# Two blocks of a projection before the norm instead of one: weights times x that is not yet normed, at five norms of a two-block network

## The chip, the cores and the metric

The kernel runs on one core of one Trainium2 chip. What counts is the time of one execution on the device in microseconds. Of three runs of the kernel before the median is 1563.91 us (1560.41 to 1564.23). Engines are named as in the profile: TensorE is PE, its weight loads PEld, VectorE is DVE, ScalarE is ACT, GpSimd is POOL, SyncE (SP) issues the weight transfers.

## The reference

One sequence of 256 tokens with 1024 features goes through two blocks. All of it is float32. The first has a convolution branch and a state-space branch, then a gated feed-forward part. The second has a gated-delta mixer (gdn) and a gated-linear mixer (gla), each followed by a squared-relu MLP. Cut to the places that the change touches:

```python
# first block
x = x + gate * (merged @ w_out)                      # w_out
h = rmsnorm(x) * (1 + scale) + shift                 # norm "ffn"
u = h @ w_ffn_in;  x = x + gate * ((silu(u1) * u2) @ w_ffn_down)
x = rmsnorm(x) * final_norm_w                        # norm "final"
# second block, i = 0 (gdn) and 1 (gla)
m = mixer_i(x)                                       # first projection: a_qkv, b_qk
x = layernorm(ALPHA * x + m)                         # norms "ln1_0", "ln1_1"
a = relu(x @ mlp_w1)                                 # mlp1_0, mlp1_1
x = layernorm(ALPHA * x + (a * a) @ mlp_w2)          # norms "ln2_0", "ln2_1"
```

## The kernel before, in words

The 256 tokens lie along the free axis, features on the partitions: x is the tile X of eight 128x256 pieces. A projection is a **section** (the list SECS): a series of 256-column blocks of weights. SP loads a block of 1 MB (8 k-tiles of 128 rows) into one of four slots of `raw`, in one order for the whole kernel (`order`), as soon as the block four places earlier has been used. Float32 precision comes from splitting weights and data in two: ScalarE makes the high part `whi` (split_hi, L463), VectorE or, in the sections with lo="gpsimd" (a_qkv is one), POOL makes the low part `wlo` (split_lo, L473), which also frees the raw slot. A block has two tiles of 128 columns (h = 0, 1); `whi` and `wlo` have four places, so two blocks. TensorE multiplies each k-tile three times (L596 hi x hi, L597 hi x lo of the data, L598 lo x hi): 48 matmuls a block, summed in one of four PSUM slots `acc` (out_slot). Some engine then evacuates the tile (acc_free).

In ffn_in some raw slots hold parts of w_ada_ffn instead (ADA_PLAN): after blocks 1, 3, 5 and 7 VectorE folds them into ADAG (L1678, L1680), which is what frees those slots.

**Norms.** Before a norm x is summed from the residual evacuations (L1971, L1975) of the section before: w_out, ffn_down, a_out, mlp2_0, b_out (BEFORE). Sections with several k-chunks per output (ffn_down, mlp2_0: four) are "long": only every fourth block ends in an evacuation. For five norms (EARLY) the first block of the next section (ffn_in, a_qkv, mlp1_0, b_qk, mlp1_1) does not wait: while the section before ends, ScalarE squares x (SQX) and writes its high part times the gain (GHI, act_first, L760, L761), VectorE the low part (GLO, low_halves, L794); TensorE (pe_early, L692, L714, L718) multiplies with these, with the sums over features for mean and variance between them (L697, L700, L703, L707), and two extra columns carry the gain and the shift through the weights. When the norm's factors NR are there, VectorE's scale_first (L857 to L864) corrects the two tiles of block 0 in PSUM.

The norm itself is norm_dve and norm_act: VectorE makes the low split of block 1 (L473), mean and variance (L928 to L931), centres x (L934, not for ffn and final), scales it (L940, SQX), runs scale_first and writes the low part HL (L954, L956); ScalarE loads a table (L880), makes the high split of block 1, the inverse root (L913, L916) and the high part HH (L907, L909). Block 1 is the first on HH: pe_first (L530, L531) does its hi matmuls as each HH piece comes, then those on HL (L537). After that split_section runs each engine through the blocks: split of block b + 1, then the evacuation of block b, then `extra`.

**What lies behind.** In a_qkv each tile is evacuated by ScalarE (L1422) and by four VectorE operations (conv, L1828); `gates` on VectorE (L2016 to L2021, with softplus, L1744 to L1756) stands after block 2's conv, and decay_sides(0) to (7) after those of blocks 3 to 10 (L2030 to L2034). L2505 on TensorE waits for the last of them. PE computes small_tok and the shift sums (pe_shift, L726, L727) after block 1. In mlp1_0 the shift sums stand after block 1, and POOL then adds the shift to X (L740). In b_qk the shift sums and the gate logits (L2684) stand after block 1, L2691 after block 2. b_v (L588) follows.

Of the kernel before, what the change touches and what calls it, by code (L numbers as in the profile page):

```python
# [20 lines left out]
P = 128  # L21
# [65 lines left out]
def program(nc, a, out):  # L87
# [46 lines left out]
    for k in ("conv_b", "conv_a", "xbc", "z", "g", "conv_out", "ssm_out", "w_out", "ffn_in", "a_qkv", "mlp1_0", "mlp1_1"):  # L134
        SEC[k].flat = True
# [70 lines left out]
    with ExitStack() as ctx:  # L206
# [77 lines left out]
        WB = at("WB", 101.75, [P, 4])  # L284
# [191 lines left out]
        def split_section(eng, split, s, evac, chain=None, per=0, extra=None):  # L476
# [29 lines left out]
        def out_slot(s, u, h):  # L506
# [6 lines left out]
            return (s.o0 + h) % 4  # L513

        def pe_first(pe, s, rhs, ready, b, u, j):

            hi_part, lo_part = ready
            for h in range(2):
                pe.wait_ge(hi_ready, 2 * b + s.t0 + h + 1)
                pe.wait_ge(raw_used, 2 * (b + s.w0) + h + 1)  # L520
                if s.name == "ffn_in":
                    pe.wait_ge(acc_free, s.o0 + 2 * h + 2)
# [28 lines left out]
        def pe_block(pe, s, rhs, tok_major=False, free=None, ready=None):  # L551

            def body(b, u, last, j, only=(0, 1)):
                k = kt_of(s, u)
                if s.name in NORM_OF and b == 0:
                    pe_early(pe, NORM_OF[s.name])
                    return
                if ready and b == (1 if s.name in NORM_OF else 0):
# [4 lines left out]
                for h in only:  # L563
                    tt = 2 * b + s.t0 + h
                    pe.wait_ge(hi_ready, tt + 1)
                    pe.wait_ge(raw_used, 2 * (b + s.w0) + h + 1)
                    if first:
# [8 lines left out]
                        else:  # L576
                            pe.wait_ge(acc_free, 2 * j + s.o0 + h + 3)
                    slot, q = (s.t0 + 2 * u + h) % 4, out_slot(s, u, h)
# [46 lines left out]
        for n, (name, mean, src) in enumerate(norm_list):  # L625
# [8 lines left out]
        PARTS = {"ffn": 0, "final": 1, "ln1_0": 2, "ln2_0": 4, "ln1_1": 6}  # L634
        RANK = {name: i for i, name in enumerate(EARLY)}
        BEFORE = {"ffn": "w_out", "final": "ffn_down", "ln1_0": "a_out", "ln2_0": "mlp2_0", "ln1_1": "b_out",
                  "ln2_1": "mlp2_1"}

# [30 lines left out]
        def parts(name):  # L669

            if SEC[BEFORE[name]].chunks > 1:
                return [NR[:, 0]], [SQX[:, 0]]
            return [XP[:, i] for i in range(3)], [SQX[:, i] for i in range(3)]

        def width(name):
            return T if name == "final" else WIDE

        def pe_early(pe, name):
# [3 lines left out]
            place_ = [(h, (s.t0 + h) % 4, out_slot(s, 0, h)) for h in range(2)]  # L682
            for h in range(2):
                pe.wait_ge(hi_ready, s.t0 + h + 1)
                pe.wait_ge(raw_used, 2 * s.w0 + h + 1)
            late = 2 if SEC[BEFORE[name]].chunks > 1 else 0
# [2107 lines left out]
```

## Time and profile before

| | before |
|---|---|
| median of 3 runs | 1563.91 us |
| profiled execution | 1569.33 us, span 1567.6 us |
| PE busy | 1430.1 us (91%) |
| DVE busy | 1011.0 us (64%) |
| ACT busy | 773.8 us (49%) |
| POOL busy | 404.8 us (26%) |
| granted TensorE clock, mean | 0.959 |
| DMA | 223.74 MB, 143 GB/s |

Shares are means over stages with different limits. The chain that ended last runs through PE for 72% of the span, through DVE for 13%, ACT for 6%. The five places lie at 453 to 475 us (ffn), 650 to 712 (final), 963 to 988 (ln1_0), 1161 to 1209 (ln2_0) and 1348 to 1373 (ln1_1) of the span. All times below count from the span's start.

### The profile page before, as it was taken

The page shows a single profiled execution, that of the slowest core. Times are in us where ns is not written, and L with a number is a line of the kernel's source. Part 1 is how long each engine was busy: PE and PEld are TensorE (multiplying, and loading weights), DVE is VectorE, ACT ScalarE, POOL GpSimd, SP SyncE. Part 2 cuts the span into 40 slices and gives each one's busy share as a digit, 9 for nine tenths or more (in the row PEclk, how much of TensorE's full clock was granted, in tenths as well). Part 3 has the DMA queues.
Part 4 walks back from the last instruction along what each step waited for, and adds up shares of the span by engine and source line. Part 5 has one row for each costly group of instructions (what it writes and reads, how often), then busy time and mean ns, then how long its engine had stood idle before and what let it go on. Part 6 is the DMA issues. An engine that isn't in the chain of part 4 may idle for free.

```text
span 1567.6 us, 27516 instructions
## 1 busy us (share of the span) xinstructions
PE 1430.1 (91%) x10981; PEld 1376.4 (88%) x10981; DVE 1011.0 (64%) x1726; ACT 773.8 (49%) x1211; POOL 404.8 (26%) x362
## 2 busy tenths in 40 slices
PE   4979999989898999898988889999999987999998
PEld 4979999988898999898878879999997976899997
DVE  6687868657676655579655557865464565876442
ACT  3424465574363433464573545664354643666333
POOL 1566774304300000156372401730005000200000
PEclk9889999999899999989999999999999998999999
DMA  9944553233746745635310005555552510365540
GB/s 354 363 135 148 175 162 108 82 107 120 240 153 221 227 158 161 202 85 159 108 54 1 1 1 161 158 183 171 187 161 83 179 38 14 122 188 189 176 146 28
DMA packets 202480, 223.74 MB, mean 143 GB/s; under 512 B 7608, under 2 KB 197723, under 8 KB 200317
## 3 DMA queue, kind: packets, MB, share of 16 engines
q1 hardware_dynamic: 201072, 220.67, 43.8%
q8 instruction: 80, 1.31, 0.4%
q10 hardware_dynamic: 1293, 1.47, 0.3%
q14 instruction: 35, 0.29, 0.1%
HBM read 221.07 MB, written 1.05 MB: 142 GB/s over the span
## 4 chain that ended last, share of the span: by engine, by line
PE 72%; DVE 13%; ACT 6%; POOL 3%; issue 3%; DMA 2%; SPq 0%; DVEq 0%; ACTq 0%; POOLq 0%
PE acc L596 18%; PE acc L598 17%; PE acc L597 17%; DVE GB L1828 2%; DVE wlo L473 1%; ACT whi L463 1%; POOL H L967 1%; PE acc L537 1%; PE acc L530 1%; DMA raw<-in_w_ffn_in 1%; DVE SQX L940 1%; DMA XIN<-in_x 1%; PE acc L531 1%; POOL AM L1194 1%; PE pm L2359 1%
## 5 line engine op out<-in xcount | busy, mean ns | idle before, releaser
L596 PE MATMUL acc<-HH,whi 128*128 128x256 f32 x1744 | 501.2, 287 | 29.1 <-issue 9.1
L463 ACT ACTIVATE whi<-raw 128x1024 fp32r<-128x1024 f32 (+2 forms) x380 | 378.7, 1029 | 242.1 <-PE acc L598 194.1
L597 PE MATMUL acc<-HL,whi 128*128 128x256 f32 x1744 | 496.0, 284 | 0.0
L598 PE MATMUL acc<-HH,wlo 128*128 128x256 f32 x1744 | 495.9, 284 | 0.0
L473 DVE TENSOR_TENSOR wlo<-raw,whi 128x1024 fp32r<-128x1024 f32 (+2 forms) x292 | 340.0, 1196 | 208.5 <-ACT whi L463 205.8
L596 PEld LDWEIGHTS acc<-HH,whi 128*128 128x128 f32 x1744 | 334.4, 192 | 36.6 <-issue 28.6
L597 PEld LDWEIGHTS acc<-HL,whi 128*128 128x128 f32 x1744 | 334.0, 192 | 0.3 <-issue 0.2
L598 PEld LDWEIGHTS acc<-HH,wlo 128*128 128x128 f32 x1744 | 333.6, 191 | 0.0
L473 POOL TENSOR_TENSOR wlo<-raw,whi 128x1024 fp32r<-128x1024 f32 x88 | 213.6, 2446 | 397.9 <-DVE wlo L473 246.6
L596 PE MATMUL acc<-HIDH,whi 128*128 128x256 f32 x688 | 195.7, 284 | 6.4 <-ACT whi L463 4.5
L597 PE MATMUL acc<-HIDL,whi 128*128 128x256 f32 x688 | 195.4, 284 | 0.0
L598 PE MATMUL acc<-HIDH,wlo 128*128 128x256 f32 x688 | 195.3, 284 | 0.0
L596 PEld LDWEIGHTS acc<-HIDH,whi 128*128 128x128 f32 x688 | 132.7, 193 | 7.0 <-issue 7.0
L597 PEld LDWEIGHTS acc<-HIDL,whi 128*128 128x128 f32 x688 | 132.9, 193 | 0.0
L598 PEld LDWEIGHTS acc<-HIDH,wlo 128*128 128x128 f32 x688 | 132.8, 193 | 0.0
L1814 DVE SCALAR_TENSOR_TENSOR pm<-UP,par,pm 128x256 f32<-128x256 f32 x158 | 66.9, 481 | 0.0
L530 PE MATMUL acc<-HH,whi 128*128 128x256 f32 x128 | 40.9, 342 | 15.7 <-ACT HH L909 6.7
L1561 ACT ACTIVATE TMP<-acc 128x256 f32<-128x256 f32 x60 | 23.0, 384 | 63.8 <-PE acc L598 58.9
L1194 POOL TENSOR_TENSOR AM<-ATT,gm 128x512 f32<-128x512 f32 x28 | 38.4, 1394 | 59.3 <-DVE ATT L2114 42.0
L2195 DVE TENSOR_TENSOR TMQ<-TMP 128x256 f32<-128x256 f32 x64 | 28.9, 452 | 37.4 <-ACT HIDH L1564 37.4
L1828 DVE SCALAR_TENSOR_TENSOR GB<-acc,par,GB 128x254 f32<-128x254 f32 (+1 forms) x96 | 45.1, 480 | 9.2 <-ACT GB L1422 6.4
L967 POOL TENSOR_SCALAR X<-SQX,par 128x256 f32<-128x256 f32 x8 | 8.2, 1035 | 161.0 <-DVE SQX L940 161.0
(554 smaller groups left out, 2541.7 us busy)
## 6 DMA issues: line engine op xcount, KB each, us to landing
raw<-in_mlp_w SPq DMA_DIRECT2D x64, 1024.0 KB, 5.3
raw<-in_w_in SPq DMA_DIRECT2D x36, 1024.0 KB, 5.3
raw<-in_w_ffn_in SPq DMA_DIRECT2D x22, 1024.0 KB, 5.3
raw<-in_a_w_in SPq DMA_DIRECT2D x16, 1024.0 KB, 5.7
raw<-in_b_w_in SPq DMA_DIRECT2D x12, 1024.0 KB, 5.3
raw<-in_w_ada_mix SPq DMA_DIRECT2D x8, 1024.0 KB, 7.1
ADR<-in_w_ada_ffn SPq DMA_DIRECT2D x8, 1024.0 KB, 11.5
raw<-in_w_ssm_out SPq DMA_DIRECT2D x8, 1024.0 KB, 5.2
```

The source lines that it names most:

```text
L463: act.activation(whi[:, (s.t0 + 2 * u + h) % 4, 0:k], raw[:, place(s, b, u) % 4, 0:k, h * P:h * P + P], ACT.Copy).then_inc(hi_ready, 1)
L473: v.tensor_tensor(wlo[:, slot, 0:k], raw[:, place(s, b, u) % 4, 0:k, h * P:h * P + P], whi[:, slot, 0:k].bitcast(F32), ALU.subtract).then_ ...
L530: pe.matmul(acc[:, q, 0:T], whi[:, slot, i], hh, start=i == 0, stop=False)
L596: pe.matmul(acc[:, q, 0:T], whi[:, slot, i], hh, start=first and i == 0, stop=False)
L597: pe.matmul(acc[:, q, 0:T], whi[:, slot, i], hl, start=False, stop=False)
L598: m = pe.matmul(acc[:, q, 0:T], wlo[:, slot, i], hh, start=False, stop=final and i == k - 1)
L967: pool.tensor_scalar(dst[:, k], SQ[name][:, k], shift(k) if shift else 0.0, None, ALU.add)\
L1194: pool.tensor_tensor(AM[u][:, lv % 2].rearrange("p (s c) -> p s c", s=4), ATT[u][:], mask, ALU.mult).then_inc(am_ok, 1)
L1561: act.activation(TMP[:, q], acc[:, out_slot(s, u, h), 0:T], ACT.Relu, bias=evac_bias(s, b, u, h))\
L1814: c.tick(v.scalar_tensor_tensor(ACC[:, i] if w_ == CW - 1 else sum_, src, wt, sums.get(i, sum_), ALU.mult, ALU.add))
L1828: ins = v.scalar_tensor_tensor(d_, x_, pc(w, i + 24 * tap), d_, ALU.mult, ALU.add)
L2195: c.link(v.tensor_tensor(TMQ[:, q], TMP[:, q], TMP[:, q], ALU.mult))
```

## The change

Blocks 0 and 1 of the five sections are now both multiplied with GHI and GLO in pe_early; the first block on HH is block 2. WB grows to eight columns, scale_first gets a block number and runs twice, for block 0 ahead of HL and for block 1 behind it. ScalarE's table load and the high splits of blocks 0 and 1 move ahead of the last evacuations; the high split of block 2 comes after HH. VectorE makes the low split of block 1 after the variance, of block 2 between scale_first(0) and HL, and of block 3 in block 1's turn of split_section. The order of pe_early changes: hi and lo weights on the first six k-tiles, and the last two last. Of the sums, the parts over the first k-tiles (pe_parts) are multiplied before the last tile of the section before, and short sections have one summed part each instead of three. `mid` runs between the two last residual evacuations, so that pieces 6 and 7 of x are handled one by one; the low halves of a long section are made in two groups of three. ffn_down and mlp2_0 become `flat` (written out, not looped) and rotate their output tiles over four slots. The first three low splits of a_qkv go from POOL to VectorE. gates, small_tok, the shift sums and the gate logits come one block later, and so do decay_sides; act_shift of mlp1_0 two.

```diff
-    for k in (..., "w_out", "ffn_in", "a_qkv", "mlp1_0", "mlp1_1"):
+    for k in (..., "w_out", "ffn_in", "ffn_down", "a_qkv", "mlp1_0",
+              "mlp2_0", "mlp1_1"):
...
                 for h in range(2):
-                    if s.name in NORM_OF and eng is not nc.gpsimd and b == 0:
+                    if s.name in NORM_OF and b in (0, 2):
                         continue
-                    if split and not last:
+                    if split and s.name in NORM_OF and b == 1:
+                        split(eng, s, 3, 3, h)
+                    elif split and not last:
                         split(eng, s, b + 1, u + 1, h)
...
                         evac(b, u, h, j)
+                        if mid and last and h == 0:
+                            mid()
...
-            return (s.o0 + h) % 4
+            return (s.o0 + h + (2 * j if s.flat else 0)) % 4
...
-                if s.name in NORM_OF and b == 0:
-                    pe_early(pe, NORM_OF[s.name])
+                if s.name in NORM_OF and b < 2:
+                    if b:
+                        pe_early(pe, NORM_OF[s.name])
                     return
-                if ready and b == (1 if s.name in NORM_OF else 0):
+                if ready and b == (2 if s.name in NORM_OF else 0):
                     pe_first(pe, s, rhs, ready, b, u, j)
...
+                    if s.name in NORM_BEFORE and last and h == 1:
+                        pe_parts(pe, NORM_BEFORE[s.name])
...
+            tiles = [(2 * b + h, (s.t0 + 2 * b + h) % 4, out_slot(s, b, h)) for b in range(2) for h in range(2)]
...
+            open_(first)
+            with_hi(first, whi, range(6))
             if mean:
...
+            with_hi(first, wlo, range(6))
...
             m.then_inc(n_sum, 1)
...
+            open_(second)
+            with_hi(second, whi, range(6))
+            pe.wait_ge(raw_used, 2 * s.w0 + 2)
+            with_hi(second, wlo, range(6))
+            for tile in (first, second):
+                with_lo(tile, range(6))
+            for tile in (first, second):
+                with_hi(tile, whi, (6, 7))
+                with_hi(tile, wlo, (6, 7))
+                with_lo(tile, (6, 7)).then_inc(w_used, 1)
+            for tile in tiles[2:]:
+                open_(tile)
+                with_hi(tile, whi, range(8))
+                with_lo(tile, range(7))
+                pe.wait_ge(raw_used, 2 * s.w0 + tile[0] + 1)
+                with_hi(tile, wlo, range(8))
+                with_lo(tile, (7,)).then_inc(w_used, 1)
...
+                if b == last - 1:
+                    act.preload_act_table_set("natural_log_exp_and_others")
+                    for h in range(2 if name == "ffn" else 0):
+                        split_hi(act, e, 0, 0, h)
+                elif b == last:
+                    split_hi(act, e, 1, 1, 0)
+                    act_first(act, name, (6, 7))
+                    split_hi(act, e, 1, 1, 1)
...
+                if b == last - 1 and name in ("ffn", "final"):
+                    v.wait_ge(raw_used, 2 * e.w0)
+                    for h in range(2):
+                        split_lo(v, e, 0, 0, h)
+
+            def mid():
+                if not is_long(name):
+                    v.wait_ge(n_sq, 8 * n + 6)
+                    v.tensor_tensor(SQX[:, 4], SQX[:, 4], SQX[:, 5], ALU.add).then_inc(part_ok, 1)
+                low_halves(v, c, name, (6,))
...
+            if name in EARLY:                      # norm_act, at its end
+                for h in range(2):
+                    split_hi(act, SEC[EARLY[name]], 2, 2, h)
...
+            if e:                                  # norm_dve, after the variance
+                for h in range(2):
+                    split_lo(v, e, 1, 1, h)
...
-            if name in EARLY:
-                scale_first(v, c, name)
+            if e:
+                scale_first(v, c, name, 0)
+                for h in range(2):
+                    split_lo(v, e, 2, 2, h)
             for k in range(DT):                    # HL
...
+            if e:
+                scale_first(v, c, name, 1)
...
-            lo_section(SEC["a_qkv"])
+            s = SEC["a_qkv"]
+            for b in range(3, s.nb):
+                if b == 3:
+                    pool.wait_ge(raw_used, 2 * (s.w0 + b))
+                for h in range(2):
+                    split_lo(pool, s, b, b % 4, h)
...
-                if b == 2:
+                if b == 3:
                     gates()
-                elif 3 <= b < 11:
-                    decay_sides(b - 3)
+                elif 4 <= b < 12:
+                    decay_sides(b - 4)
```

## Rows read from the trace of the kernel before

**Rows 1.** TensorE's waits over the span: waiter, releaser, us in total, times, longest.

```profile
PE acc L530 <- ACT HH L909: 6.7, 4, 2.8
...
PE acc L596 <- DVE GB L1828: 5.1, 1, 5.1
PE acc L692 <- DVE X L1975: 4.9, 1, 4.9
```

**Rows 2.** Windows of TensorE alone: us, busy (instructions), granted clock, DMA share, GB/s.

```profile
990.00:1060.00 70.00, 70.00 (x592) 1.00 0.62 194
1184.00:1187.00 3.00, 3.00 (x16) 0.50 0.14 19
```

**Rows 3.** Timeline of DVE at the norm ffn: start, us, what, [idle before <-releaser].

```profile
457.08 2.36 DVE L473 TENSOR_TENSOR wlo<-raw,whi 128x1024 fp32r<-128x1024 f32 x2 [1.77 <-ACT whi L463]
459.35 3.25 DVE L940 SCALAR_TENSOR_TENSOR SQX<-X,MOD,NR 128x256 f32<-128x256 f32 x8
...
463.58 3.25 DVE L956 SCALAR_TENSOR_TENSOR HL<-SQX,MOD,HH 128x256 fp32r<-128x256 f32 x8
466.74 2.35 DVE L473 TENSOR_TENSOR wlo<-raw,whi 128x1024 fp32r<-128x1024 f32 x2
...
472.35 1.28 DVE L1680 SCALAR_TENSOR_TENSOR ADAG<-raw,cs,ADAG 128x1024 f32<-128x1024 f32 x1
```

**Rows 4.** The chain that ended last, in ffn_in: start, us, what.

```profile
473.66 5.17 DMA raw<-in_w_ffn_in
...
487.49 5.25 DMA raw<-in_w_ffn_in
```

**Rows 5.** Timeline of TensorE where that chain lets go.

```profile
516.58 0.36 PE L596 MATMUL acc<-HH,whi 128*128 128x256 f32 x1 [1.41 <-ACT whi L463]
```

**Rows 6.** Timeline of DVE in a_qkv, around gates.

```profile
696.06 0.38 DVE L2016 TENSOR_TENSOR spt<-pm,gab 128x16 f32<-128x16 f32 x2
...
698.71 7.84 DVE L1753 SCALAR_TENSOR_TENSOR spt<-spt,spt 128x32 f32<-128x32 f32 x7
...
709.88 3.98 DVE L1828 SCALAR_TENSOR_TENSOR GB<-acc,par,GB 128x254 f32<-128x254 f32 x8 [0.16 <-DVE gd L2021]
```

**Rows 7.** Timeline of POOL in the same stretch.

```profile
698.52 4.74 POOL L473 TENSOR_TENSOR wlo<-raw,whi 128x1024 fp32r<-128x1024 f32 x2 [11.08 <-ACT whi L463]
```

**Rows 8.** Timeline of TensorE behind a_qkv.

```profile
756.22 0.49 PE L2505 MATMUL pm<-maskf,LF 128*128 128x128 f32 x2 [2.22 <-DVE LB L2031]
```

**Rows 9.** Groups by line, 964 to 988 us: xcount | busy us, mean ns | idle before.

```profile
L697 PE MATMUL pm<-SQX,maskf 128*128 128x256 f32 x6 | 1.5, 379 | 0.0
```

**Rows 10.** Timeline of DVE at the norm ln1_0.

```profile
972.03 2.73 DVE L934 SCALAR_TENSOR_TENSOR X<-pm,X 128x256 f32<-128x256 f32 x8
974.68 4.28 DVE L940 SCALAR_TENSOR_TENSOR SQX<-X,par,NR 128x256 f32<-128x256 f32 x8
...
980.98 3.25 DVE L956 SCALAR_TENSOR_TENSOR HL<-SQX,par,HH 128x256 fp32r<-128x256 f32 x8
...
985.73 2.35 DVE L473 TENSOR_TENSOR wlo<-raw,whi 128x1024 fp32r<-128x1024 f32 x2
```

**Rows 11.** Timeline of TensorE at ln1_0: the shift sums follow block 1.

```profile
985.46 0.28 PE L726 MATMUL pm<-HH,maskf 128*128 128x256 f32 x1
```

**Rows 12.** Timeline of TensorE at ln1_1: the first matmul of block 2.

```profile
1372.25 0.36 PE L596 MATMUL acc<-HH,whi 128*128 128x256 f32 x1 [1.44 <-issue]
```

**Rows 13.** Timeline of TensorE at ln2_0.

```profile
1169.75 2.08 PE L718 MATMUL acc<-GLO_ln,whi 128*128 128x258 f32 x16
1174.63 0.36 PE L530 MATMUL acc<-HH,whi 128*128 128x256 f32 x1 [2.81 <-ACT HH L909]
...
1180.46 4.67 PE L537 MATMUL acc<-HL,whi 128*128 128x256 f32 x16 [0.60 <-DVE HL L956]
...
1187.94 3.64 PE L2684 MATMUL pm<-X,ws 128*32 128x256 f32 x16
```

**Rows 14.** Timeline of TensorE: the first matmul of b_v.

```profile
1209.02 0.39 PE L588 MATMUL acc<-whi,HH 128*128 128x256 f32 x1 [0.47 <-ACT QK L1580]
```

More of the change, by code:

```diff
@@ L133, in program @@
     SEC = {s.name: s for s in SECS}
-    for k in ("conv_b", "conv_a", "xbc", "z", "g", "conv_out", "ssm_out", "w_out", "ffn_in", "a_qkv", "mlp1_0", "mlp1_1"):
+    for k in ("conv_b", "conv_a", "xbc", "z", "g", "conv_out", "ssm_out", "w_out", "ffn_in", "ffn_down", "a_qkv", "mlp1_0",
+              "mlp2_0", "mlp1_1"):
         SEC[k].flat = True
@@ L633, in program @@
         XC0 = {"conv": 0, "ln1_0": 8, "ln2_0": 17, "ln1_1": 26, "ln2_1": 35}
-        PARTS = {"ffn": 0, "final": 1, "ln1_0": 2, "ln2_0": 4, "ln1_1": 6}
+        PARTS = {"ffn": 0, "final": 2, "ln1_0": 3, "ln2_0": 6, "ln1_1": 8}
         RANK = {name: i for i, name in enumerate(EARLY)}
@@ L667, in norm_pe, with is_long, pe_parts @@
                 keep_busy(pe, 4)
[L669 to L673, printed above, removed]
+        def is_long(name):
+            return SEC[BEFORE[name]].chunks > 1
         def width(name):
             return T if name == "final" else WIDE
+        def pe_parts(pe, name):
+            mean = NORM[name][1]
+            pe.wait_ge(part_ok, PARTS[name] + (2 if mean else 1))
+            if mean:
+                pe.matmul(pm[:, 0, 0:T], ones, NR[:, 0] if is_long(name) else XP[:, 0], start=True, stop=False)
+            pe.matmul(pm[:, 1, 0:T], ones, SQX[:, 0], start=True, stop=False)
         def pe_early(pe, name):
@@ L681, in pe_early, with with_hi, with_lo, open_ @@
             o0 = SEC[BEFORE[name]].o0 + 4
[L682 to L686, printed above, removed]
[L687 to L689 removed]
+            tiles = [(2 * b + h, (s.t0 + 2 * b + h) % 4, out_slot(s, b, h)) for b in range(2) for h in range(2)]
+            def with_hi(tile, weights, ks):
+                i, slot, q = tile
                 for k in ks:
                     pe.wait_ge(g_hi, g + k + 1)
[L692 to L697 removed]
+                    pe.matmul(acc[:, q, 0:w], weights[:, slot, k], hi[:, k, 0:w],
+                              start=k == 0 and weights is whi, stop=False)
+            def with_lo(tile, ks):
+                i, slot, q = tile
+                for k in ks:
+                    pe.wait_ge(g_lo, g + k + 1)
+                    m = pe.matmul(acc[:, q, 0:w], whi[:, slot, k], lo[:, k, 0:w], start=False, stop=k == 7)
+                return m
+            def open_(tile):
+                i = tile[0]
+                pe.wait_ge(hi_ready, s.t0 + i + 1)
+                pe.wait_ge(acc_free, s.o0 + i + 1)
+            first, second = tiles[0], tiles[1]
+            open_(first)
+            with_hi(first, whi, range(6))
             if mean:
[L699 to L700 removed]
                 for k in (6, 7):
@@ L704, in pe_early @@
                 m.then_inc(n_mean, 1)
+            pe.wait_ge(raw_used, 2 * s.w0 + 1)
+            with_hi(first, wlo, range(6))
+            if not is_long(name):
+                pe.wait_ge(part_ok, PARTS[name] + (3 if mean else 2))
+                pe.matmul(pm[:, 1, 0:T], ones, SQX[:, 4], start=False, stop=False)
             for k in (6, 7):
```

208 lines of the change are left out of this document (100 added, 108 removed).

## The prediction

> **What bounds the kernel now.** I read four views, in this order. First the waits of TensorE over the whole span: who ends its idle times. TensorE is the engine that is nearly always busy, so only its idle times, its slow stretches and work taken off it can move the end. Of the joints that the diff touches, the first block on the normed x waited for ScalarE's HH four times (6.7 us in all), GHI_final's first matmul waited 4.9 us for the last residual, and a_qkv waited 5.1 us once for VectorE [rows 1]. Second, windows: undisturbed, 592 matmuls take 70 us, 0.118 us each, so a block of 48 takes 5.7 us; in a disturbed stretch 16 fall in 3 us at a granted clock of 0.50, 0.19 to 0.21 us each [rows 2]. Third, VectorE's order of work around each norm, since it makes everything TensorE waits for there. Fourth, in ffn_in, the chain of waits, which does not run through TensorE at all: an ADAG step on VectorE frees a raw slot, a 5.2 us transfer fills it, ScalarE and VectorE split it, VectorE evacuates, and does the next ADAG steps [rows 4].
>
> **The plan of the change.** In each of five places TensorE gets 48 more matmuls (5.7 us) that need no norm and are moved ahead of the first block that does. Their total number stays. That covers the wait for HH. But VectorE is the engine that follows the norm, and it gets more to do before it is through: scale_first for a second block, and the low split of block 2 ahead of HL. So for each place I lay VectorE's row durations end to end in the new order and see what TensorE meets. Starts that no row gives are sums of such durations, good to about 1 us.
>
> **ffn.** Before: low split of block 1 (2.36), eight scalings (3.25), scale_first (1.0, from 462.60 to 463.58), eight HL (3.25), low split of block 2 (2.35, to 469.09), two evacuations and a first ADAG step (3.3), the second (1.3), which ends at 473.63 [rows 3]. In the new order a second scale_first (1.1) and the low split of block 3 (2.36) stand before that ADAG; the wait for the high split of block 2, which ScalarE now does after HH, adds 0.6; the table load, moved ahead of the first high split, and two small additions make the scalings start 0.3 late; block 1's split no longer waits. Sum 1.1 + 2.4 + 0.6 + 0.3 = 4.4, with link overheads 4.7: the ADAG ends near 478.3. TensorE itself would be 2 us early at the end of block 2. That is worth nothing: its next weights need the slot that this ADAG frees. The loop has a period of 13.8 us (473.66 to 487.49) for two blocks that cost TensorE 11.4, with no matmul in it [rows 4], and it only lets go at 516.58, where TensorE still idles 1.41 us before it [rows 5]. So the shift is carried through whole: **+4.7 us** (bounds 2.4, the moved split alone, and 6).
>
> **final.** The 4.9 us wait goes: VectorE no longer does six low halves and three sums in one piece ahead of the last residuals, and TensorE, with four rotating output slots, may start before them. POOL's low splits of blocks 0 and 1 go to VectorE, which is not blocked then. TensorE's sums end near 661.3, 132 matmuls follow (15.7 us), and block 2 is done near 677. But a_qkv is then VectorE's. gates() with its small operations took from 696.06 to 709.72, because each of the two-input ones met a POOL split: seven L1753 take 7.84 us, while the first two operations of gates, ahead of the split, take 0.38 together [rows 6, 7]. It is now done after conv of block 3 instead of block 2 (3.98 each, [rows 6]). VectorE's queue is: convs of blocks 0 to 3 from 677 on, 16 us, gates at 693.1, 13.7 us as before, end 706.9 against 709.7: 2.8 us won. From there to the last decay side, which releases L2505 at 756.22 [rows 8], the same eight convs and eight decay sides follow in either kernel, 46.5 us of VectorE, so L2505 comes 2.8 us earlier. No conv is behind it any more (it had been 3.97 us ahead of ScalarE's last silu and its exponentials), I take 1.2 us for that; TensorE idles longer before it, and I give back 0.7 for clock. **-3.3 us** (bounds 0 and -8, the latter if gates meets no POOL work).
> The Trainium skill ("SBUF — State Buffer", section "Who interferes with whom") says that VectorE and GpSimd take their common port as a lock for a whole instruction, and the later one is blocked: the rows of L1753 agree. By that rule what counts is which instruction POOL has running when gates comes.
>
> **ln1_0.** Three fewer sum matmuls (six instructions take 1.5 us, [rows 9]: 1.3 us off), and two of the rest moved before the last tile. The sums end near 969.0. TensorE then has 84 matmuls, 10.0 us: free at 979.0. VectorE: the low split of block 1 stays ahead of the centring (2.36, 2.73), scalings 4.28, scale_first 2.1, so until 981.0, as before; then the low split of block 2, its first half ready at 982.2 [rows 10]. **So TensorE's new wait is for a low split, 3.2 us.** Block 2 lasts until 988.0 (before, block 1 ended at 985.46 [rows 11]), and with the shift sums (1.9) block 2 is done at 989.9, against 985.46 + 1.9 + 5.7 = 993.1. Behind block 2's split VectorE has HL 3.25, scale_first 2.1, two evacuations 1.6 (984.2 to 985.73), then the split of block 3, first half at 991.7. Block 3 so starts 1.4 us early. The 3.2 us of idling will probably bring half clock for a while, which the wait at block 3 hides for the most part; POOL's X additions now meet a VectorE that is behind. I take **-0.7 us** (bounds -3 and +2).
>
> **ln1_1.** The same without shift sums: waits of 2.6 us before block 2 and 3.6 before block 3, which starts at 1376.4 where before it would have started at 1378.0 (block 2 at 1372.25 [rows 12] plus 5.7): -1.6, and 0.6 for clock. **-1.0 us** (-2 to +2).
>
> **ln2_0.** Before, TensorE idled 2.81 and 0.60 us, and its 16 lo matmuls took 4.67 instead of 2.08 [rows 13]; two slow stretches follow. Block 3 ended at 1208.5, the next block began at 1209.02 [rows 14]. After: sums at 1167.5, 84 matmuls until 1177.5, low split of block 2 at 1180.7 (scale_first 3.0 here), block 2 until 1186.5, shift sums 1.9, gate logits 3.6 [rows 13], block 3 (its split is ready at 1189.4, so no second wait) until 1197.8, L2691 3.8: 1201.6. That is 6.9 us early; half clock after the 3.2 us of idling costs 1.5 to 3. **-4.9 us** (-7 to -2).
>
> **At no cost.** ffn_down and mlp2_0 written out instead of looped: TensorE has no idle time in their loops, so there is nothing to win; if fetching code stalled once, it would cost 1 to 2 us. WB and the output slots take no time.
>
> **Sum.** +4.7 - 3.3 - 0.7 - 4.9 - 1.0 = -5.2 us. The profiled execution took 1569.33 us (span 1567.6), 5.4 above the median of the runs; so 1564.1 by its own count, and 1563.91 - 5.2 = 1558.7 for the median.
>
> **Rivals.**
> *VectorE eats the cover.* Slower. The place is the wait for the low split before blocks 2 and 3. If VectorE's queue (scale_first, split, HL, scale_first, evacuation) is longer by 2 us than I have it, in all five places, then ln1_0 and ln1_1 each cost 1, final gives 0, ln2_0 gives 2.5, and ffn costs 6: +5.5, 1569. It decides from where block 3 starts later than before, 1.4 us beyond my schedule of ln1_0. For it: the longest wait of the sort before was already VectorE's, 5.1 us in a_qkv [rows 1]. Against: the durations are plain rows of the same operations.
> *The slot chain gives way.* If ADAG's delay is caught up in ffn_in, that place gives -2 and not +4.7: 1552. For it: VectorE idles over 4 us per turn for the transfer. Against: the idling is inside the loop, and nothing else of the loop gets shorter [rows 4].
> *POOL is idle while gates runs.* Final gives -8: 1554. For it: TensorE runs two blocks ahead of VectorE, so POOL may be done. Against: ScalarE's exponential waits for gates, and its next high split stands behind it, so POOL starts within gates.
> *Clock.* [rows 2, 13] show half clock after idling of 3.4 us. My schedule has five waits of 2.6 to 3.6 us; at 1.5 us each, three not hidden beyond those that I counted: +4.5, 1563. The Trainium skill ("TensorE: Matmul & The Clock Gate", "HAM oscillation — how this bites in real kernels") speaks against waits of this sort between bursts; the rows agree.
>
> **Chances.** My forecast 0.45 (own range 1555 to 1563), VectorE 0.15, slot chain 0.10, POOL idle 0.15, clock 0.15. The range, 1551 to 1567, leaves out half of the slower case. About 0.3%, 4.7 us, is what a measurement of this kernel can tell from no change. Below 1559.2: 0.28 of my own case and the slot and POOL cases, 0.53. Above 1568.6 or near it: 0.12. The rest 0.35.
>
> **What would show it.** ADAG L1680 of block 1 ends near 478.3, and TensorE's wait at 516.58 comes 4 to 5 us late. No wait of L692 for X. TensorE's first matmuls on HH wait for wlo (VectorE), not for HH. gates ends near 707, L2505 starts near 753 plus the shift of ffn. b_v's first matmul comes some 5 us sooner after the end of mlp2_0. Wrong would be: an ffn_in that is not later, a ln2_0 without gain, or half clock throughout the third blocks.

## The result, and the profile after

The changed kernel is slower: 1581.05 us, median of four runs (1578.04 to 1586.44), against 1564.02 us for the kernel before; the ratio is 1.0109, 95% interval 1.0087 to 1.0131. My forecast was 1558.7, with a range of 1551 to 1567. The profiled execution took 1580.77 us, with a span of 1579.0. All medians here are of the fast runs; one slow run in ten of adag1 is left out.

From the page of the changed kernel: busy time (share of the span) and instructions by engine, then the granted clock in 40 slices.

```profile
PE 1419.7 (90%) x10967; PEld 1372.9 (87%) x10967; DVE 1021.2 (65%) x1770; ACT 772.6 (49%) x1211; POOL 392.1 (25%) x356
...
PEclk9889999999899999989899999999999998999999
```

TensorE is busy for 10 us less than before and the span is 11.4 us longer, so TensorE idles more. The waits of TensorE over the whole span say where (waiter, releaser, us in total, times, longest); of the first view of before, this is what answers to [rows 1]:

```profile
PE acc L604 <- ACT whi L464: 10.9, 4, 5.7
...
PE acc L535 <- DVE GB L1899: 9.4, 1, 9.4
PE acc L535 <- ACT TMP L1632: 9.1, 1, 9.1
...
PE pm L2581 <- DVE LB L2107: 7.3, 1, 7.3
```

The first matmuls on the normed x (now L535, block 2) hardly wait for this norm's HH any more (1.7 us once, L963, where the list of before has 6.7 for its L909). But two of them wait 9.4 and 9.1 us for the *evacuation of an output tile*, a releaser that is in none of my cases. L2581 (the L2505 of before) waits 7.3 us where it waited 2.2 [rows 8].

The two traces differ by 11.45 us. By the starts of the same instructions, one trace of each kernel, it falls to the stages so (us; the difference is that of the stage alone). The first mark is a residual evacuation of w_out, ahead of the norm ffn; L2505 and L2581 are the decay products, which wait for the last decay side.

| stage, up to | before | after | difference | forecast |
|---|---|---|---|---|
| ahead of the norm ffn | 446.41 | 448.42 | +2.0 | 0 |
| ffn, to ffn_down's first matmul | 594.57 | 600.14 | +3.6 | +4.7 |
| final, to L2505 / L2581 | 756.22 | 768.50 | +6.7 | -3.3 |
| ln1_0, to mlp2_0's first matmul | 1069.59 | 1087.04 | +5.2 | -0.7 |
| ln2_0, to b_out's first matmul | 1325.86 | 1335.67 | -7.6 | -4.9 |
| ln1_1, to mlp2_1's first matmul | 1454.46 | 1465.79 | +1.5 | -1.0 |
| mlp2_1 and the end | 1567.60 | 1579.05 | +0.1 | 0 |

The medians are 17 us apart, 5.5 more than the traces: the profiled execution of before happened to lie 5.3 us above its median, that of after at its median.

**final.** Timeline of VectorE (start, us, what, [idle before <-releaser]), of POOL and of TensorE in the changed kernel; it answers to [rows 6 to 8].

```profile
676.27 7.06 DVE L1016 TENSOR_TENSOR HL<-SQX,HH 128x256 fp32r<-128x256 f32 x8
683.26 0.75 DVE L920 TENSOR_TENSOR acc<-acc,NR 128x256 f32<-128x256 f32 x2
683.92 7.85 DVE L1899 SCALAR_TENSOR_TENSOR GB<-acc,par,GB 128x254 f32<-128x254 f32 x16
693.83 3.98 DVE L1899 SCALAR_TENSOR_TENSOR GB<-acc,par,GB 128x254 f32<-128x254 f32 x8 [2.05 <-ACT GB L1493]
704.61 2.04 DVE L1899 SCALAR_TENSOR_TENSOR GB<-acc,par,GB 128x254 f32<-128x254 f32 x4 [6.80 <-ACT GB L1493]
707.46 2.04 DVE L1899 SCALAR_TENSOR_TENSOR GB<-acc,par,GB 128x254 f32<-128x254 f32 x4 [0.81 <-ACT GB L1493]
709.41 0.46 DVE L2092 TENSOR_TENSOR spt<-pm,gab 128x16 f32<-128x16 f32 x2
...
676.65 5.07 POOL L474 TENSOR_TENSOR wlo<-raw,whi 128x1024 fp32r<-128x1024 f32 x2 [267.12 <-ACT whi L464]
...
686.20 0.55 PE L535 MATMUL acc<-HH,whi 128*128 128x256 f32 x1 [9.42 <-DVE GB L1899]
694.07 3.65 PE L2435 MATMUL pm<-ws,SQX 128*128 128x32 f32 x32
768.50 0.80 PE L2581 MATMUL pm<-maskf,LF 128*128 128x128 f32 x2 [7.27 <-DVE LB L2107]
```

Two early blocks fill all four output slots. Block 2 needs block 0's first slot, whose taps (the convolution's four VectorE operations per tile, L1899) stand on VectorE behind the low halves HL. So TensorE idles until 686.20. Its small products (L2435) and shift sums come after block 2 and ahead of block 3, and VectorE, which needs block 3's tiles before it may begin the gates, idles 2.05 + 6.80 + 0.81 us among the taps. The gates begin at 709.41, against 696.06. The low halves themselves are late too: two of the eight take 2.57 and 2.56 us beside POOL's split, the other six 0.42 each.

**ln1_0.** The same view of VectorE, ScalarE and TensorE there, answering to [rows 10, 11].

```profile
996.67 3.25 DVE L1018 SCALAR_TENSOR_TENSOR HL<-SQX,par,HH 128x256 fp32r<-128x256 f32 x8
...
1001.13 0.76 DVE L920 TENSOR_TENSOR acc<-acc,NR 128x256 f32<-128x256 f32 x2
...
1001.26 0.47 ACT L1632 ACTIVATE TMP<-acc,WB 128x256 f32<-128x256 f32 x1 [6.32 <-DVEq L2265]
...
1001.99 0.55 PE L535 MATMUL acc<-HH,whi 128*128 128x256 f32 x1 [9.06 <-ACT TMP L1632]
```

Here the slot is freed by ScalarE's relu of block 0, and that waits for DVEq L2265: an increment, `v.sem_inc(hid_lo, 4)`, that hands out four free places of TMP at the start of VectorE's mlp(0). It stands behind the whole norm, both scalings included. Block 0 had been scaled since 994.5. Before, block 1 found its slots free and nobody on the path waited for that increment.

**ffn.** The chain of waits there (start, us, what), which answers to [rows 4]:

```profile
477.70 0.77 DVE ADAG L1749
478.47 0.02 issue
478.49 1.30 DVE ADAG L1751
479.79 0.02 issue
479.80 5.07 DMA raw<-in_w_ffn_in
484.87 0.02 issue
484.90 1.06 ACT whi L464
```

**ln2_0 and ln1_1.** TensorE's waits ahead of block 2 are for low splits, as forecast; they answer to [rows 12, 13].

```profile
1196.52 0.56 PE L535 MATMUL acc<-HH,whi 128*128 128x256 f32 x1 [2.97 <-DVE wlo L474]
...
1377.36 0.36 PE L535 MATMUL acc<-HH,whi 128*128 128x256 f32 x1 [2.16 <-DVE wlo L474]
1386.94 0.36 PE L604 MATMUL acc<-HH,whi 128*128 128x256 f32 x1 [3.41 <-DVE wlo L474]
```

### The profile page after: what moved, and what is told of

The parts are those of the page before. It is cut to its first block, busy times and chain, and to the rows that moved or that the text cites. A ratio compares the mean times of both kernels' runs of the same rounds, so it can differ in the third digit from the quotient of the medians.

```text
span 1579.0 us, 27235 instructions
## 1 busy us (share of the span) xinstructions
PE 1419.7 (90%) x10967; PEld 1372.9 (87%) x10967; DVE 1021.2 (65%) x1770; ACT 772.6 (49%) x1211; POOL 392.1 (25%) x356
## 4 chain that ended last, share of the span: by engine, by line
PE 71%; DVE 15%; ACT 5%; POOL 3%; issue 3%; DMA 2%; SPq 0%; DVEq 0%; ACTq 0%; POOLq 0%
PE acc L604 17%; PE acc L605 16%; PE acc L606 16%; DVE wlo L474 2%; DVE GB L1899 2%; PE acc L535 1%; POOL H L1031 1%; PE acc L536 1%; PE acc L702 1%; DMA raw<-in_w_ffn_in 1%; ACT whi L464 1%; DMA XIN<-in_x 1%; PE acc L542 1%; DVE HL L1018 1%; DVE SQX L1000 1%
## 5 line engine op out<-in xcount | busy, mean ns | idle before, releaser
L604 PE MATMUL acc<-HH,whi 128*128 128x256 f32 x1664 | 480.1, 288 | 33.8 <-POOL wlo L474 8.1
L605 PE MATMUL acc<-HL,whi 128*128 128x256 f32 x1664 | 475.0, 285 | 0.0
L606 PE MATMUL acc<-HH,wlo 128*128 128x256 f32 x1664 | 473.9, 285 | 0.0
L474 DVE TENSOR_TENSOR wlo<-raw,whi 128x1024 fp32r<-128x1024 f32 (+2 forms) x298 | 347.8, 1199 | 190.8 <-ACT whi L464 187.4
L604 PEld LDWEIGHTS acc<-HH,whi 128*128 128x128 f32 x1664 | 319.9, 192 | 39.9 <-issue 29.2
L605 PEld LDWEIGHTS acc<-HL,whi 128*128 128x128 f32 x1664 | 319.9, 192 | 0.3 <-issue 0.2
L606 PEld LDWEIGHTS acc<-HH,wlo 128*128 128x128 f32 x1664 | 319.7, 192 | 0.0
L474 POOL TENSOR_TENSOR wlo<-raw,whi 128x1024 fp32r<-128x1024 f32 x82 | 198.0, 2433 | 424.0 <-ACT whi L464 420.6
L535 PE MATMUL acc<-HH,whi 128*128 128x256 f32 x128 | 41.3, 347 | 33.6 <-DVE GB L1899 9.4
L535 PEld LDWEIGHTS acc<-HH,whi 128*128 128x128 f32 x128 | 31.8, 248 | 35.5 <-issue 30.0
L1899 DVE SCALAR_TENSOR_TENSOR GB<-acc,par,GB 128x254 f32<-128x254 f32 (+1 forms) x96 | 45.1, 480 | 12.4 <-ACT GB L1493 9.7
L1265 POOL TENSOR_TENSOR AM<-ATT,gm 128x512 f32<-128x512 f32 x28 | 38.4, 1393 | 59.1 <-DVE ATT L2190 41.8
```

What stands on the lines that cost most here:

```text
L474: v.tensor_tensor(wlo[:, slot, 0:k], raw[:, place(s, b, u) % 4, 0:k, h * P:h * P + P], whi[:, slot, 0:k].bitcast(F32), ALU.subtract).then_ ...
L535: pe.matmul(acc[:, q, 0:T], whi[:, slot, i], hh, start=i == 0, stop=False)
L604: pe.matmul(acc[:, q, 0:T], whi[:, slot, i], hh, start=first and i == 0, stop=False)
L605: pe.matmul(acc[:, q, 0:T], whi[:, slot, i], hl, start=False, stop=False)
L606: m = pe.matmul(acc[:, q, 0:T], wlo[:, slot, i], hh, start=False, stop=final and i == k - 1)
L1265: pool.tensor_tensor(AM[u][:, lv % 2].rearrange("p (s c) -> p s c", s=4), ATT[u][:], mask, ALU.mult).then_inc(am_ok, 1)
```

## The experiments

Each kernel is an edit of the changed one. The table gives stages from one trace of each (us): ffn and final run from the first matmul on GHI to the marks of the table above, ln1_0 from the decay products to mlp2_0's first matmul. So final begins later here than in the table above, and what the change saves ahead of GHI_final (4.7 us; the wait of 4.9 us there is gone) lies outside it. The same code differs between traces by up to 0.6 us in ffn, 2.1 in final and 1.7 in ln1_0.

| kernel | ffn | final | ln1_0 | span |
|---|---|---|---|---|
| before | 141.5 | 93.1 | 313.4 | 1567.6 |
| after | 144.3 | 104.5 | 318.5 | 1579.0 |
| nop | 144.2 | 104.6 | 312.6 | 1572.6 |
| pms | 144.1 | 102.9 | 311.4 | 1569.1 |
| one | 140.1 | 91.8 | 314.6 | 1565.3 |
| ln2 | 140.2 | 91.9 | 314.6 | 1558.4 |
| gates1 | 144.6 | 93.2 | 318.3 | 1573.7 |
| adag1 | 139.3 | 102.4 | 318.8 | 1571.6 |
| pe1 | 144.4 | 97.1 | 319.0 | 1566.4 |
| dve1 | 144.1 | 100.4 | 317.8 | 1571.1 |
| fixed | 139.5 | 92.9 | 312.6 | 1553.0 |
| best | 139.9 | 91.1 | 311.3 | 1554.4 |
| fixed_pool | 139.9 | 87.5 | 310.9 | 1551.0 |

### nop: the increment goes ahead of the norm

```
+            v.sem_inc(hid_lo, 4)
             norm_dve(v, c, "ln1_0", par_col("ln1_g"), par_col("ln1_b"))
 ...
-                if k == 0:
-                    v.sem_inc(hid_lo, 4)
```

> The changed kernel with one edit: VectorE gives the first four counts of hid_lo before the normalisation of ln1_0 and not behind it. Theory A (the second early block has taken the last free output slots, so block 2 of mlp1_0 waits for block 0's relu, and that relu waits for these four counts, which stand behind VectorE's low halves and the scaling of block 1): TensorE's wait of 9.06 us ahead of line 535 in ln1_0 falls to about 3.8 us, that is to the low split of block 2 (its end was 996.75, TensorE was free at 992.93); the kernel gains 5 us, 1581 to about 1576. All other sections stay within 0.5 us. Rival B (VectorE's backlog as such): the wait stays above 8 us, no gain. Rival C (the half clock is the cost): as A, but the half-clock window at 998.1 goes with the wait and the gain is 7 to 8 us.

Measured: 1571.36 us, ratio to the kernel before 1.0056 (1.0025 to 1.0088). TensorE's wait in ln1_0, in the trace of this kernel:

```profile
995.61 0.36 PE L535 MATMUL acc<-HH,whi 128*128 128x256 f32 x1 [2.75 <-DVE wlo L474]
```

The wait is 2.75 us instead of 9.06, and its releaser is now the low split, the one that I had forecast for this place. The stage is 6.0 us shorter (318.5 to 312.6). Theory A holds here; rival B falls. That the matmul runs at 0.36 us and not 0.55 shows the half clock gone with the wait, so C's part is included in those 6 us, not beside them. The medians moved by 9.7 us, more than A's 5 and C's 8, while the two traces differ by 6.5; the changed kernel has only four runs (1578.04 to 1586.44). So the price of a cause is read from its stage here and below, and the medians only say that it is there.

### pms: block 0 in other banks

```
+        def out_tile(s, b, u, h):
+            return pm[:, 2 + h] if in_pm(s, b) else acc[:, out_slot(s, u, h)]
 ...
+                if in_pm(s, 0):
+                    pass
+                    pe.wait_ge(acc_free, SEC["a_qkv"].o0 + 4 + 2)
                     small_tok(ws2, SQX, ba_p)
```

> The changed kernel, but block 0 of a_qkv and of mlp1_0 lies in the two banks of the other PSUM tensor that are free there, so that block 2 finds its output slots free; everything else, the order on every engine too, is as changed (TensorE's small products into one of these banks wait for the evacuation of block 0 first). Theory A: the waits of 9.42 us (final) and 9.06 us (ln1_0) ahead of line 535 fall to about 0.5 and 3.8 us; in final block 2 then waits 2 to 3 us for the low halves of h, which end at 683.3, and VectorE begins the gates near 700 instead of 709.4. In all 9 plus 5 us less, 1581 to about 1567. Rival B (VectorE's backlog): the waits move one block on, block 3 waits for block 1's evacuation as long, and the total falls by less than 4 us.

Measured: 1573.13 us, ratio 1.0049 (1.0026 to 1.0071). In ln1_0 it does what nop does. In final the slot wait is gone, and the stage is only 1.6 us shorter, which is no more than the same code differs by. TensorE and VectorE there:

```profile
681.18 3.32 PE L551 MATMUL acc<-HL,whi 128*128 128x256 f32 x13 [1.20 <-DVE HL L1025]
687.16 1.03 PE L2444 MATMUL pm<-ws,SQX 128*128 128x32 f32 x4 [2.66 <-DVE GB L1908]
...
700.69 2.04 DVE L1908 SCALAR_TENSOR_TENSOR GB<-acc,par,GB 128x254 f32<-128x254 f32 x4 [5.91 <-ACT GB L1502]
703.54 2.04 DVE L1908 SCALAR_TENSOR_TENSOR GB<-acc,par,GB 128x254 f32<-128x254 f32 x4 [0.81 <-ACT GB L1502]
705.50 0.46 DVE L2101 TENSOR_TENSOR spt<-pm,gab 128x16 f32<-128x16 f32 x2
```

This was my theory's miss. The 9.4 us that the list of waits shows were not what held the stage: VectorE still idles 5.91 us for block 3's tiles, since on TensorE the small products and the shift sums still come before block 3: 6.9 us in the changed kernel, near 10 here, most of it at half clock (the 32 small products take 7.01 us instead of 3.65). (2.66 us of the delay is the wait that this edit itself adds.) Whoever wants to know what a stage costs has to ask what VectorE's gates wait for, not what TensorE waits for.

### one, ln2: how many early blocks, and where

Each use of "two blocks" takes its number from a table:

```
+    NB = {'ffn': 1, 'final': 1, 'ln1_0': 1, 'ln2_0': 1, 'ln1_1': 1}
 ...
-                if s.name in NORM_OF and b < 2:
+                if s.name in NORM_OF and b < NB[NORM_OF[s.name]]:
```

> The changed kernel with one early block per norm instead of two, in all five places; the other parts of the change stay (four rotating slots for the long sections, flat sections, residuals and sums tile by tile, the table load and the high split moved). Theory A (the second block is what costs, by 3.7 + 6.7 + 5.0 + 1.5 us, and brings 7.6 in ln2_0): the total is about 1564 to 1570, ffn, final and ln1_0 back at the spans of the kernel before within 2 us each, ln2_0 about 7 us longer than changed. Rival D (the other parts of the change cost too): above 1575.

> As the run with one early block everywhere, but two early blocks at ln2_0 alone. Theory A: 7 to 8 us less than that run, near 1558 to 1562, faster than both kernels. Rival: the gain in ln2_0 came from the longer lead that the slower sections before it had given the DMA; then this run is within 3 us of the one with one block everywhere.

Measured: one 1563.30 us, ratio 0.9987 (0.9970 to 1.0004); ln2 1556.89 us, ratio 0.9960 (0.9931 to 0.9990). The other parts of the change cost nothing and bring nothing, together, that can be told from no change; rival D falls. The second block costs 4.2 us in ffn, 12.7 in final and 3.9 in ln1_0, and brings its gain in ln2_0, 6.8 us in the traces and 6.4 in the medians. ln2 beats both kernels. Its ln2_0 stage is as long as the changed kernel's (249.0 and 248.6), so a longer lead of the DMA, that run's rival, is not what brings the gain.

### gates1, pe1, dve1: where the gates stand in a_qkv

pe1 has the first hunk (TensorE), dve1 the others (ScalarE and VectorE), gates1 all:

```
 def gates(b):                       # TensorE: small products, shift sums
-    if b == 2:
+    if b == 1:
 def qkv_more(b):                    # ScalarE
-    elif b == 3:
+    elif b == 2:
 def qkv_more(b):                    # VectorE
-    if b == 3:
+    if b == 2:
         gates()
-    elif 4 <= b < 12:
-        decay_sides(b - 4)
+    elif 3 <= b < 11:
+        decay_sides(b - 3)
```

> The changed kernel with one edit in a_qkv: the small products and shift sums of TensorE come after block 1, and ScalarE's and VectorE's gate work after block 2, the block numbers of the kernel before; two early blocks and the slots stay. The run with block 0 in other banks took the slot wait of final away and left the stage as long as it was (102.9 us from the first early matmul to the decay products, changed 104.5, one early block 91.8), so my theory of the slots has fallen for final. Theory E (the gates' place): VectorE bounds a_qkv from the gates to the last decay side, 59 to 60 us in every kernel, and the change made it begin the gates after block 3's taps, and block 3 itself comes behind 7.6 us of small products on TensorE. With the old place the gates begin near 696 instead of 709.4, the last decay side lies ahead of block 11's taps again, and the decay products start near 756 instead of 768.5: 11 to 13 us less in all. Rival B (VectorE's additional work, a scaling and two low splits, is what costs): less than 6 us.

> The changed kernel with half of the edit on the gates: TensorE's small products and shift sums come after block 1, the gate work of ScalarE and VectorE stays behind block 3. It parts the 11.3 us that the whole edit took from the stage final (104.5 to 93.2 us from the first early matmul to the decay products). Theory E says that both halves count: here the small products fill TensorE's wait for the output slots, block 3 follows block 2 at once, VectorE's taps of blocks 0 to 3 run almost without a gap, and the gates begin 4 us (one block's taps) later than with the whole edit: stage 95 to 97 us. Rival (only the engines' order behind the gates counts): 103 to 105 us.

> The other half: the gate work of ScalarE and VectorE behind block 2, TensorE's small products still behind block 2 as changed. TensorE still waits for block 0's taps, the small products end near 698 and the shift sums near 701 in the changed kernel's times, ScalarE's sigmoid follows, and the gates begin near 702 instead of 709.4: stage 98 to 99 us. Rival (TensorE's order is what counts): 103 to 105 us.

Measured: gates1 1566.41 us, ratio 1.0031 (0.9996 to 1.0065); stage 93.2 us. pe1 97.1 us and dve1 100.4 us, from one execution each; their bands were 95 to 97 and 98 to 99, so both halves count; dve1's 4.1 us are about twice the scatter of this stage, pe1's 7.4 more than three times. VectorE's taps and the start of the gates, first in pe1, then in dve1:

```profile
680.12 7.86 DVE L1899 SCALAR_TENSOR_TENSOR GB<-acc,par,GB 128x254 f32<-128x254 f32 x16
688.87 5.93 DVE L1899 SCALAR_TENSOR_TENSOR GB<-acc,par,GB 128x254 f32<-128x254 f32 x12 [0.89 <-ACT GB L1493]
695.59 2.04 DVE L1899 SCALAR_TENSOR_TENSOR GB<-acc,par,GB 128x254 f32<-128x254 f32 x4 [0.79 <-ACT GB L1493]
697.54 0.46 DVE L2092 TENSOR_TENSOR spt<-pm,gab 128x16 f32<-128x16 f32 x2
```

```profile
691.17 3.98 DVE L1899 SCALAR_TENSOR_TENSOR GB<-acc,par,GB 128x254 f32<-128x254 f32 x8 [2.18 <-ACT GB L1493]
700.42 0.38 DVE L2092 TENSOR_TENSOR spt<-pm,gab 128x16 f32<-128x16 f32 x2 [5.26 <-ACT bet L1507]
```

In pe1 TensorE does the small products while it would have idled for the slot, and the taps of blocks 0 to 3 run with 1.7 us of gaps: this is the packed queue on which my forecast for final rested. In dve1 the gates wait 5.26 us for ScalarE's sigmoid, which hangs on TensorE's late sums. With both, the slot wait is covered and the gates come a block earlier. The spans of gates1 and the changed kernel differ by only 5.3 us, since gates1's trace is 7.7 us longer in ln2_0, which this edit doesn't touch (see the last section).

### adag1: ffn's slot is freed first

```
+            def ffn_pre(b):
+                for n in SEC["ffn_in"].ada[b] if b == 1 else ():
+                    ada_rest(n - 8)
-            split_section(v, split_lo, SEC["ffn_in"], ffn_up, extra=ffn_more)
+            split_section(v, split_lo, SEC["ffn_in"], ffn_up, extra=ffn_more, pre=ffn_pre)
```

> The changed kernel with one edit in ffn_in: VectorE does the ADAG step of block 1 ahead of the low split of block 3 and of the two evacuations. Theory (the step frees the weight slot on which the next load waits): the step ends near 475 instead of 479.8, the wait of 5.75 us at 487.4 falls to about 1.5 us, although block 3 now waits 2 us for its low split, and ffn_down begins 3.5 to 4.5 us sooner than the 600.14 of the changed kernel. Rival (the load was late for another reason, its queue or the high split): less than 1 us.

Measured: 1571.96 us, ratio 1.0032 (1.0002 to 1.0063); the stage is 139.3 instead of 144.3 us. Two views of TensorE in this trace (timeline):

```profile
476.77 0.36 PE L606 MATMUL acc<-HH,whi 128*128 128x256 f32 x1 [2.54 <-DVE TMQ L2064]
489.04 0.36 PE L606 MATMUL acc<-HH,whi 128*128 128x256 f32 x1 [0.64 <-issue]
```

The wait of 5.75 us is gone. Block 3 waits 2.5 us, about as long as expected, but not for its low split: the releaser is TMQ L2064, the evacuation of block 1, so here too an early block's output slot holds TensorE. The stage gains more than that costs, 4.9 us for a forecast of 3.5 to 4.5, since the chain that sets it runs through the weight slot. The rival falls.

### fixed, best: what the causes add up to

fixed holds nop, gates1 and adag1; best holds nop and NB = 2 in ln1_0, ln2_0 and ln1_1, 1 in ffn and final.

> Three edits in one: the counts of hid_lo ahead of ln1_0's normalisation, the gates in their old place, and ADAG's step of block 1 first; two early blocks everywhere. If the three causes are separate their gains add, 6 + 12 + 4 us: 1581 to about 1559, as fast as or faster than the kernel before by 0.3%. If one lies behind another, above 1565.

> Two early blocks in ln1_0, ln2_0 and ln1_1 and one in ffn and final, with the counts of hid_lo first. From the runs so far, against the run with two blocks at ln2_0 alone (1556.9): ln1_0 2 us less, ln1_1 1 us less, about 1554, that is 0.7% faster than the kernel before. Rival (the second block in ln1_0 and ln1_1 is worth nothing): 1557.

Measured: fixed 1556.45 us, ratio 0.9944 (0.9924 to 0.9963); best 1555.23 us, ratio 0.9928 (0.9903 to 0.9953). The three causes are separate: each stage of fixed is as in the run with its own edit, and against the changed kernel the three stages give 4.8 + 11.6 + 5.9 = 22.3 us of the 26.0 between the spans, for a forecast of 22. Most of the rest is ln2_0, 2.8 us shorter in this trace. The change, with three statements in other places, is faster than the kernel before. The intervals of fixed and best overlap, so which is better is not settled; 1555.23 also lies between best's forecast of 1554 and its rival's 1557 and decides for neither.

### fixed_pool: POOL waits for VectorE's low halves

```
                 if b == 3:
                     pool.wait_ge(raw_used, 2 * (s.w0 + b))
+                    pool.wait_ge(n_hl, 8 * HN["final"] + 8)
```

> The kernel with the three edits, and POOL begins its low split of block 3 of a_qkv only when all low halves of h are there. If POOL's running split is what makes VectorE's eight low halves take 7.07 us instead of 3.25, they take 2.8 to 3.3 us now, TensorE's wait of 3.0 us for them goes, and the gates begin 3 us sooner: 1556.5 to about 1553.5. Rival: POOL's split only moves onto something else that VectorE does with two inputs from SBUF, and the total stays within 1 us.

Measured: 1551.64 us, ratio 0.9907 (0.9879 to 0.9935). That is the lowest median of all, from four runs; the interval still overlaps those of fixed and best, so what shows the gain is the stage. VectorE and POOL in its trace:

```profile
670.30 2.77 DVE L1018 TENSOR_TENSOR HL<-SQX,HH 128x256 fp32r<-128x256 f32 x8
673.64 11.95 DVE L1902 SCALAR_TENSOR_TENSOR GB<-acc,par,GB 128x254 f32<-128x254 f32 x24
685.50 0.38 DVE L2098 TENSOR_TENSOR spt<-pm,gab 128x16 f32<-128x16 f32 x2
...
673.20 4.76 POOL L474 TENSOR_TENSOR wlo<-raw,whi 128x1024 fp32r<-128x1024 f32 x2 [262.75 <-DVE HL L1018]
```

The eight low halves take 2.77 us where they took 7.07 beside POOL's split. The gain, 4.8 us in the medians and 5.4 in the stage, is more than the 3 that I expected: the gates begin 5.8 us sooner after the first early matmul than in fixed, 4.3 us from the low halves and the rest from a gap of 1.58 us among the taps, which now run all 24 on end. TensorE's wait of 3.03 us for the low halves is gone. POOL's split runs beside the taps (L1902) and does not slow them: those that lie beside it take 0.47 to 0.49 us each, and so do those behind it. The taps have one input in PSUM, the low halves both in SBUF. The Trainium skill ("SBUF — State Buffer", section "Who interferes with whom") says this: two SBUF inputs on VectorE contend with a GpSimd instruction that reads SBUF, one input doesn't. Both rows agree.

## Why the prediction was wrong

The two traces differ by +11.4 us where the sum gave -5.2. Of these 16.7 us, 10.0 are final's and 5.9 are ln1_0's; the other stages err by 2.0, -1.1, -2.7 and 2.5 and nearly cancel.

**final, the step that failed: "convs of blocks 0 to 3 from 677 on, 16 us, gates at 693.1".** I queued VectorE's taps end to end, as if TensorE were ahead of it. My 677 is about 682.5 on the time axis of the changed trace (the sums end 5.5 us later there), so the gates should have begun at 698.6; they began at 709.41, 10.8 us later. VectorE's gaps among the taps are 9.7 us, the taps' late start 1.4. The gaps come from two things that I didn't lay out. First, TensorE's block 2 needs block 0's output slot. My sum let its 48 matmuls follow the 84 early ones at once ("132 matmuls follow (15.7 us), and block 2 is done near 677"); it was done at 694.1, 11.6 us after that place of the changed axis. I wrote that the slots "take no time" because I had looked at the rotation in ffn_down and mlp2_0 alone; in the places with two early blocks it is the other way round, all four are full. Second, I never placed the small products (3.65 us) and the shift sums between block 2 and block 3 in a_qkv, although I did so for ln1_0 and ln2_0. The trace of before had the warning: its taps stand still behind the same small work, too (timeline of VectorE in the kernel before):

```profile
691.26 2.04 DVE L1828 SCALAR_TENSOR_TENSOR GB<-acc,par,GB 128x254 f32<-128x254 f32 x4 [5.63 <-ACT GB L1422]
```

pe1, in which both fall into the gap, starts the gates at 697.54, with the early matmuls 3.8 us sooner than in the changed kernel: 2.7 us off my schedule. What follows the start of the gates was right: gates took 13.7 us as before, and from their start to the decay products it took 59.1 us, where before it was 60.2 and the forecast 59.8.

A third thing is missing in the sum. I took POOL's splits of blocks 0 and 1 away as a relief for VectorE; before, one of them had stretched the eight scalings (5.97 us instead of 3.25). But its split of block 3 now meets the low halves, and fixed_pool shows what that costs: 5.4 us of the stage.

The share of each: TensorE's part put back brings 7.4 us of final (pe1), the other part 4.1 (dve1), both 11.3. Taking the slot wait alone away brought 1.6, within the scatter of 2.1, and at most 4.3 if the 2.66 us that this edit adds are counted back. So the order of the small work is shown as the cause of most of the 11.3; the slot wait counts because that work stands behind it.

**ln1_0, the step that failed: "So TensorE's new wait is for a low split, 3.2 us."** True once the slot is free: 2.75 us in nop, and the stage is then 0.8 us shorter than before, for a forecast of -0.7; with a scatter of 1.7 us that agrees but doesn't confirm it. What I missed is a wait that is nobody's data: relu's permission to use TMP, an increment that stands behind the norm in VectorE's order. The list of waits of before showed no such releaser on TensorE, because block 1 had free slots of its own.

**ffn: right.** ADAG's step of block 1 ended at 479.8, forecast 478.3 and 2.0 for what came late ahead of the norm; the stage +3.6, forecast +4.7; and adag1 shows that this step's place is the cause.

**ln2_0: right in kind, the size not settled.** The wait is 2.97 us (forecast 3.2) on the split that I named, and the gain 7.6 (forecast 4.9, bounds 2 and 7). What I took off for clock is what varies most. Windows of TensorE behind that wait, in the changed kernel and then in gates1, 233 matmuls each (us, busy, granted clock, DMA share, GB/s):

```profile
1196.00:1231.00 35.00, 33.97 (x233) 0.95 0.39 121
```

```profile
1184.00:1223.00 39.00, 38.41 (x233) 0.83 0.35 108
```

In one trace a mean of 0.95 and 35 us, in the other 0.83 and 39: after the same wait the chip ran longer at 1.2 GHz instead of 2.4. Over the whole stage it is more. It takes 256.3 us in before and 255.8 in one; in the eleven traces with two early blocks at ln2_0 it takes 245.8 (fixed) to 256.3 (gates1), with a median of 248.9. So the gain is 7 us as a rule, 10 at best, 4 in best and fixed_pool, and nothing in gates1, though all wait 2.8 to 3.0 us in that place. My bounds of 2 and 7 were too narrow on both sides, and the 7.6 of one trace is not the size of the gain.

**ln1_1: not settled.** Forecast -1.0, measured +1.5. The waits are as forecast (2.16 and 3.41 us for 2.6 and 3.6). From b_out's first matmul to mlp2_1's, before took 128.6 us; the changed kernel and its edits with two blocks there took 127.8 to 130.4, those with one block at ln1_1 129.5 and 129.6, in the middle of the rest.

**The rivals.** "VectorE eats the cover" came nearest in time (1569) and named "the wait for the low split before blocks 2 and 3". But it priced two more microseconds of work in each of five places; what the runs show is an order of work, in final and in ln1_0. Its test, block 3 later than before in ln1_0, was met for another reason. None of the rivals had the output slots in it, and so the chance of a slower kernel, 0.12, was too small: I had listed what fills VectorE and not what each engine *holds* while it waits.

## What to carry to other kernels

Work pulled ahead of a dependency keeps its output buffer until the dependency is met: count the slots that it holds, and follow the next user of each slot back to its evacuation, over every semaphore that the evacuating engine waits for, those that only hand out permission too. When a block is added ahead of a section, everything that hangs on a block number behind it (small products, gates, increments) moves by a block in the order of its engine; place each again rather than adding to the numbers. And a long wait in the list of waits is not yet the price of a stage: take it away without changing anything else, and see whether the end moves.

## What I had not expected of the hardware

A POOL split of 5.07 us (two instructions, 2.58 and 2.52) stretches VectorE's eight two-input low halves from 2.77 to 7.06 us, and not evenly: two of them take 2.57 and 2.56, about one POOL instruction each, six stay at 0.42. Taps with one PSUM input stay at 0.47 to 0.49 beside the same split. And the granted clock behind a wait of 3 us is no constant: the same code, after the same wait, took 35 us at a mean of 0.95 and 39 us at 0.83 in two traces; over the four runs of the changed kernel 0.957 went with 1578.04 us and 0.951 with 1586.44, over the ten of gates1 0.957 with 1564.09 and 0.950 with 1580.09. So a stage read from one trace is good to some 2 us in most places, but the same code took 10.5 us more in one trace than in another in ln2_0, and up to 3.9 us more ahead of the norm ffn (the first early matmul starts at 451.95 in pe1 and at 455.87 in the changed kernel). The +2.0 us of the stage ahead of ffn is within that.
